# Two chunks' score matmuls on one weight tile in a gated linear attention head, keys packed by GpSimd

## The reference

```
f   = lb + (1 - lb) * sigmoid(fp);  k = 1 - f;  q = silu(q)
per position t, state S (128 x 128):  S = diag(f_t) S + k_t v_t^T;   o_t = q_t S
prompt: S starts at 0, t = 0..511;    samples: S is the carried state, one step each
```

## Time and profile before

| | |
|---|---|
| median of 3 runs | 1100.36 us (1100.23 to 1102.1) |
| profiled execution, span from first to last instruction | 1098.3 us |
| profiled execution, its own time | not shown apart; the median is 2.06 above the span |
| TensorE busy | 1055.9 us, 96% of the span |
| VectorE, ScalarE, GpSimd busy | 573.2, 434.1, 2.9 us |
| mean granted TensorE clock | 0.992 of full |
| moved by DMA | 100.36 MB, 91 GB/s over the span |

### The profile page before, as it was taken

One profiled execution on the slowest core, in us unless ns is written; L12 is line 12 of the kernel. 1 busy time (PEld: TensorE's weight loads), 2 busy tenths in 40 slices (PEclk: granted clock), 3 DMA queues, 4 the chain that ended last, 5 costly groups with the idle time before them and its releaser, 6 DMA issues.

```text
span 1098.3 us, 21670 instructions
## 1 busy us (share of the span) xinstructions
PE 1055.9 (96%) x8542; PEld 1034.8 (94%) x8542; DVE 573.2 (52%) x1028; ACT 434.1 (40%) x588; POOL 2.9 (0%) x9
## 2 busy tenths in 40 slices
PE   4899999999999999999999999699999999999997
PEld 3799999999999899999999999699999999999997
DVE  2666566657656788833333333855554554422223
ACT  5434335433442888822222233652323232322222
POOL 0000000000000000000000000000000000000000
PEclk9999999999999899999999999899999999999999
DMA  5533223222332233232333244033233323233321
GB/s 155 162 90 99 79 76 98 86 76 76 94 108 60 81 93 86 78 95 81 91 95 95 88 130 135 20 97 95 80 92 95 95 82 90 67 92 94 94 76 78
DMA packets 182881, 100.36 MB, mean 91 GB/s; under 512 B 3709, under 2 KB 181378, under 8 KB 182594
## 3 DMA queue, kind: packets, MB, share of 16 engines
q1 hardware_dynamic: 164898, 90.87, 27.8%
q10 hardware_dynamic: 17792, 8.91, 2.7%
q0 software_dynamic: 160, 0.15, 0.0%
HBM read 90.79 MB, written 9.13 MB: 91 GB/s over the span
## 4 chain that ended last, share of the span: by engine, by line
PE 90%; DVE 3%; ACT 2%; issue 1%; SPq 1%; DMA 1%; DVEq 0%; ACTq 0%
PE proj L1223 78%; PE pr L1322 5%; PE pi L1371 1%; DMA raw<-in_w_in 1%; PE pr L1376 1%; PE pi L1353 1%; PE pr L1345 1%; PE pi L1414 1%; PE pr L1414 1%; PE pi L1359 0%; ACT wh L358 0%; SPq L266 0%; DVE tmp L1122 0%; DVE acts L1110 0%; DVE raw L1202 0%
## 5 line engine op out<-in xcount | busy, mean ns | idle before, releaser
L1223 PE MATMUL proj<-acts,wh 128*128 128x260 f32 x4928 | 810.7, 287 | 15.5 <-DVE acts L1110 9.2
L1223 PEld LDWEIGHTS proj<-acts,wh 128*128 128x128 f32 x4928 | 679.9, 190 | 23.7 <-DVE acts L1110 10.8
L1223 PE MATMUL proj<-acts,wl 128*128 128x260 f32 x2464 | 498.5, 284 | 0.0
L1223 PEld LDWEIGHTS proj<-acts,wl 128*128 128x128 f32 x2464 | 381.9, 190 | 0.0
L720 DVE TENSOR_TENSOR wl<-raw,wh 128x1024 fp32r<-128x1024 f32 (+2 forms) x164 | 190.8, 1163 | 278.7 <-ACT wh L358 278.6
L358 ACT ACTIVATE wh<-raw 128x1024 fp32r<-128x1024 f32 (+2 forms) x164 | 165.6, 1010 | 358.9 <-PE proj L1223 350.5
L1322 PE MATMUL pr<-tmp 128*128 128x64 f32 (+1 forms) x512 | 66.4, 272 | 3.2 <-DVE tmp L947 3.2
L1322 PEld LDWEIGHTS pr<-tmp 128*128 128x128 f32 x512 | 62.9, 192 | 4.0 <-DVE tmp L947 3.4
L805 DVE TENSOR_TENSOR tmp<-tmp 128x256 f32<-128x256 f32 x56 | 23.6, 422 | 25.5 <-PE pr L1322 25.4
L676 ACT ACTIVATE acts<-tmp 128x520 f32 (+1 forms) x21 | 13.4, 639 | 42.4 <-DVE tmp L1170 42.4
L673 ACT ACTIVATE tmp<-tmp 128x520 f32<-128x520 f32 x21 | 13.5, 641 | 40.0 <-DVE tmp L1161 40.0
(11 more groups left out here) (239 smaller groups left out, 721.0 us busy)
## 6 DMA issues: line engine op xcount, KB each, us to landing
raw<-in_w_in SPq DMA_DIRECT2D x64, 512.0 KB, 4.0
raw<-in_w_ffn_in SPq DMA_DIRECT2D x44, 512.0 KB, 3.8
raw<-in_w_ffn_out SPq DMA_DIRECT2D x16, 384.0 KB, 3.1
raw<-in_w_ffn_out SPq DMA_DIRECT2D x16, 320.0 KB, 2.9
tmp<-in_state_hgrn ACTq DMA_DIRECT2D x8, 512.0 KB, 4.1
out<-tmp ACTq DMA_DIRECT2D x8, 512.0 KB, 3.2
raw<-in_w_branch_a SPq DMA_DIRECT2D x8, 512.0 KB, 3.6
raw<-in_w_branch_b SPq DMA_DIRECT2D x8, 512.0 KB, 3.5
```

The source lines that it names most:

```text
L1223: o = mm(pp[par][:, hf, 0:TH], w, x[:, hf * TH:(hf + 1) * TH], start=start and n == 0, stop=stop and n == 2)
```

## The change

1. *Scores.* For levels 1 to 7 two chunks share one weight tile. POOL copies, per level, the 256 first-half keys of all chunks into a packed tile `KP` (two tiles of 128 columns: 64 keys of one chunk, 64 of another). The score of a level is then two matmuls of 128 keys by 128 queries instead of four of 128 by 64. `score` also waits for the copy (`k_pack`), and POOL's copy for the key product (`d_k1`), which DVE now does first in a level, ahead of the total and the query product, and on which the next level waits too.
2. *Layout.* So that one access pattern reaches both, the second 256 positions of `QP`, `KS`, `VT`, `FF`, `AT` lie in reverse order; `columns`, `BLOCK` and `back` undo that where order matters. Three evacuations are therefore made in three pieces instead of one (values and forget gate on ACT, queries on DVE). Masks have two variants per level: the loaded table grows from 576 to 1024 columns.
3. *PSUM.* The two halves of a projection result lie next to each other across the bank border, so that `proj` is one run of 520 columns.
4. *Samples.* `STOK` and `VBD` have 128 rows instead of 24; rows 24 to 127 are zeroed once by POOL at the start, and `outer` multiplies over all 128.

The diff, cut to what the text speaks of (matching replacements of `halves(X)` by `X` elsewhere are left out):

```diff
-        def proj(par):
-            return pp[par][:, :, 0:TH]
+        def proj(par, at=0, n=T):
+            return pp[par][:].rearrange("p a n -> p (a n)")[:, 512 - TH + at:512 - TH + at + n]
+        def view(ap, off, *dims):
+            return bass.AP(ap.tensor, ap.offset + off, [list(ap.ap[0])] + [list(d) for d in dims])
+        def back(ap, lo, hi):
+            return view(ap, hi - 1, (-1, hi - lo))
...
-        VBD, STOK = spare[0:NS, 0:NB * P], spare[0:NS, NB * P:(NB + 2) * P]
+        VBD, STOK = spare[:, 0:NB * P], spare[:, NB * P:(NB + 2) * P]
+        KP = extra[:, 0:TC]
...
+        def second_of(ap, b):
+            return view(ap, b, (TC - b, 2), (2 * b, TC // (2 * b)), (1, b))
+        def first_of(ap, b):
+            return view(ap, 0, (TC + b, 2), (2 * b, TC // (2 * b)), (1, b))
+        BLOCK = (0, 1, 3, 2)
+        def columns(ap, c):
+            return ap[:, c * P:(c + 1) * P] if c < 2 else back(ap, BLOCK[c] * P, (BLOCK[c] + 1) * P)
...
         @block.gpsimd
         def _(eng):
+            eng.memset(spare[:, 0:(NB + 2) * P].bitcast(F32), 0.0).then_inc(E("sp_zero"), 1)
+            def pack(h, i):
+                if i == 1:
+                    eng.wait_ge(E("d_f"), h + 1)
+                else:
+                    eng.wait_ge(E("d_k1"), h * 7 + (i - 1))
+                hs = 1 << (i - 1)
+                eng.tensor_copy(KP.rearrange("p (n two b) -> p n two b", two=2, b=hs),
+                   view(KS, 0, (2 * hs, P // hs), (TC + hs, 2), (1, hs))).then_inc(E("k_pack"), 1)
+            for h in range(NH):
+                for i in range(1, 8):
+                    pack(h, i)
...
-                act(halves(VT), proj(0), AF.Copy).then_inc(posted(0), 1)
+                act(VT[:, 0:TC], proj(0, 0, TC), AF.Copy)
+                act(back(VT, TC, TP), proj(0, TC, TC), AF.Copy)
+                act(VT[:, TP:T], proj(0, TP, NB), AF.Copy).then_inc(posted(0), 1)
...
-                act(halves(SIG), proj(0), AF.Sigmoid).then_inc(posted(2), 1)
+                act(SIG[:, 0:TC], proj(0, 0, TC), AF.Sigmoid)
+                act(back(SIG, TC, TP), proj(0, TC, TC), AF.Sigmoid)
+                act(SIG[:, TP:T], proj(0, TP, NB), AF.Sigmoid).then_inc(posted(2), 1)
...
             def level(h, i):
...
-                    tb = tot(b).rearrange("p (n two) -> p n two", two=2)
-                    q2, k1 = cols_of(QP[:, 0:TP], b)[:, :, 1, :], cols_of(KS[:, 0:TP], b)[:, :, 0, :]
+                    n, m = TC // (2 * b), TC // b
+                    tb, t2 = tot(b), tot(b).rearrange("p (n two) -> p n two", two=2)
+                    k1 = first_of(KS, b)
                     if i > 2:
                         ch.wait()
+                        eng.wait_ge(E("d_k1"), h * 7 + i - 2)
                     eng.wait_ge(E("d_L"), h * 8 + i - 1)
                     eng.wait_ge(E("d_take"), h * 8 + i - 1)
-                    ch.link(tt(q2, q2, tb[:, :, 0:1].to_broadcast([P, n, b]), MUL))
-                    ch.link(tt(tot(2 * b), tb[:, :, 0], tb[:, :, 1], MUL))
-                    tt(k1, k1, tb[:, :, 1:2].to_broadcast([P, n, b]), MUL).then_inc(E("d_L"), 1)
+                    tt(k1, k1, view(tb, 1, (m - 1, 2), (2, n), (0, b)), MUL).then_inc(E("d_k1"), 1)
+                    ch.link(tt(tot(2 * b), t2[:, :, 0], t2[:, :, 1], MUL))
+                    tt(second_of(QP, b), second_of(QP, b), view(tb, 0, (m + 1, 2), (2, n), (0, b)), MUL).then_inc(E("d_L"), 1)
                 take(i - 1)
...
-                tt(halves(QP), proj(1), halves(SIG), MUL).then_inc(posted(1), 1)
+                tt(QP[:, 0:TC], proj(1, 0, TC), SIG[:, 0:TC], MUL)
+                tt(back(QP, TC, TP), proj(1, TC, TC), SIG[:, TC:TP], MUL)
+                tt(QP[:, TP:T], proj(1, TP, NB), SIG[:, TP:T], MUL).then_inc(posted(1), 1)
...
             def score(h, i, prev=True):
...
+                    eng.wait_ge(E("k_pack"), h * 7 + i)
                     eng.wait_ge(E("d_L"), h * 8 + i)
...
-                n = P if i == 0 else P // 2
-                for k in range(NCH):
-                    rhs = QP[:, k * P:(k + 1) * P]
-                    if i:
-                        rhs = rhs.rearrange("p (n two b) -> p n two b", two=2, b=1 << (i - 1))[:, :, 1, :]
-                    o = mm(bank[:, k * n:(k + 1) * n], KS[:, k * P:(k + 1) * P], rhs, start=True, stop=True)
+                if i == 0:
+                    for k in range(NCH):
+                        o = mm(bank[:, k * P:(k + 1) * P], KS[:, k * P:(k + 1) * P], QP[:, k * P:(k + 1) * P], start=True, stop=True)
+                else:
+                    hs = 1 << (i - 1)
+                    n = P // (2 * hs)
+                    for k in range(2):
+                        queries = view(QP, k * P + hs, (TC - hs, 2), (2 * hs, n), (1, hs))
+                        o = mm(view(bank, k * P // 2, (P, 2), (1, P // 2)), KP[:, k * P:(k + 1) * P], queries, start=True, stop=True)
                 o.then_inc(E("p_L"), 1)
```

More of the change, by code:

```diff
@@ L424, in hg_steps @@
                     eng.wait_ge(E("d_f"), h)
-                    act(halves(SIG), proj(1), AF.Sigmoid).then_inc(E("a_sg"), 1)
+                    act(SIG, proj(1), AF.Sigmoid).then_inc(E("a_sg"), 1)
                 if not prev:
@@ L440, in hg_steps @@
                     eng.wait_ge(posted(1), 2 * h)
-                act(halves(SIG), proj(1), AF.Sigmoid).then_inc(E("a_sq"), 1)
+                act(SIG, proj(1), AF.Sigmoid).then_inc(E("a_sq"), 1)
                 if prev:
@@ L605, in branch_gate @@
                 eng.wait_ge(posted(1), j * 2 + 2 * G_MIX - 1 + part)
-                act(halves(U(2 * part)), proj(0), AF.Sigmoid).then_inc(posted(0), 1)
+                act(U(2 * part), proj(0), AF.Sigmoid).then_inc(posted(0), 1)
             def mix(j):
@@ L785, in _ @@
             eng.wait_ge(E("m_made"), NLEV)
-            def cols_of(ap, b):
-                return ap.rearrange("p (n two b) -> p n two b", two=2, b=b)
             def level(h, i):
@@ L880, in out_gate @@
                 eng.wait_ge(E("a_sg"), h + 1)
-                tt(halves(SOG), proj(1), halves(SIG), MUL).then_inc(posted(1), 1)
+                tt(SOG, proj(1), SIG, MUL).then_inc(posted(1), 1)
             def lower_bound():
@@ L991, in gelu @@
                 eng.wait_ge(E("d_hl"), n)
-                stt(halves(GG), halves(GSQ), 1.0, proj(1), ADD, MUL).then_inc(posted(1), 1)
+                stt(GG, GSQ, 1.0, proj(1), ADD, MUL).then_inc(posted(1), 1)
             def gated(n):
@@ L1074, in mix @@
                 eng.wait_ge(E("unit_done"), u0 + 2)
-                tt(halves(U(1)), proj(1), halves(U(0)), MUL).then_inc(posted(1), 1)
+                tt(U(1), proj(1), U(0), MUL).then_inc(posted(1), 1)
                 prep(u0 + 3, 3)
@@ L1081, in mix @@
                 eng.wait_ge(E("a_mhi"), j)
-                tt(halves(U(3)), proj(1), halves(U(2)), MUL).then_inc(posted(1), 1)
+                tt(U(3), proj(1), U(2), MUL).then_inc(posted(1), 1)
                 prep(u0 + 5, 1)
@@ L1137, in _ @@
             eng.wait_ge(E("unit_done"), 4 * G_FFI + 2)
[L1138 to L1139 removed]
+            cp(U(0), proj(0)).then_inc(posted(0), 1)
+            cp(U(3), proj(1)).then_inc(posted(1), 1)
             prep(4 * G_FFI + 3, 3)
@@ L1334, in turn_keys @@
             def turn_keys(h):
+                eng.wait_ge(E("d_k1"), h * 7 + 7)
                 eng.wait_ge(E("d_L"), h * 8 + 8)
@@ L1536, in _level_masks @@
         tc = np.arange(P // 2)[None, :]
-        t = tc // hs * 2 * hs + hs + tc % hs
-        m = (s // (2 * hs) == t // (2 * hs)) & (s % (2 * hs) < hs)
-        out.append(m.astype(np.float32))
+        t = tc // hs * 2 * hs + tc % hs
+        same = s // (2 * hs) == t // (2 * hs)
+        out.append((same & (s % (2 * hs) < hs)).astype(np.float32))
+        out.append((same & (s % (2 * hs) >= hs)).astype(np.float32))
     return np.ascontiguousarray(np.concatenate(out, axis=1))
```

63 lines of the change are left out of this document (33 added, 30 removed).

## The result

The changed kernel takes 1094.84 us (median of four runs, 1093.56 to 1095.81) against 1100.3: 5.5 us less, a ratio of 0.9947 with a 95% interval of [0.9932, 0.9963]. The forecast was 1087.3, 13.1 faster. Direction and range held; less than half of the gain came.

The account below looks back on a forecast made before the run. TensorE was taken to bound the eight heads. Scores (-8.0) and outer products (-5.1) took 13.1 us off the span of 1098.3, giving 1085.2; with 2.06 added, the time was 1087.3, range 1081 to 1107.

Parts of the forecast that it names:

- The outer products: Outer products over 128 rows: 0.25 us each for 0.43, pairs behind them back to 1.50; 0.64 a head, 5.1 in all.
- The score itself: Levels 1 to 7: four records for eight, a score costing 0.41 us where it was 0.81.
- wide-score rival: Scores of levels 1 to 7: stepped columns cost double, a score stays at 0.81 us; 1103 in all; chance 0.08.
- Level 4: Behind VectorE's half of the weight split: key product at 8.11, score at 9.36 after score 0, TensorE still for 0.95 us.
- K: Time from the key product's start until TensorE sees packed keys: 1.25 us, bounds 0.96 and 1.51.
- the chain behind a score: Score to next score where TensorE waits: 0.92 us to VectorE's start plus K, 2.17; used for scores 6 and 7.
- The rest of the level hides beside the pack.: In each level, total and query product run beside POOL's pack; queries are ready 0.96 to 1.22 us after the key product's start.
- The start and the hop: VectorE starts 0.92 us after a score, 0.10 of it for the added wait; each hop between engines takes 0.12.
- One sign of failure that was named: The forecast fails if TensorE waits for POOL at each of levels 2 to 7.
- The first rival: At each level the pack can't run beside VectorE and waits for the query product: 1098.6, or 1091 with a 0.40 pack; chance 0.30.
- The long pack: POOL's pack is long: each 0.1 us of K beyond 1.25 costs about 0.4 a head, up to 1109.7; chance 0.17.
- The rest at nothing: Split evacuations, query pieces, larger masks and contiguous PSUM views cost nothing; uncovered, each would cost 0.15 to 0.3 us a head.

Follow-up runs that it names:

- order alone: The kernel before with 128-row outer products and the best kernel's order of VectorE's work, but eight-record scores and no packing: 1095.28 us, ratio 0.9955.
- two-column copy: The changed kernel with each of POOL's packing copies cut to two columns, so the keys aren't packed: 1087.17 us, ratio 0.9876.
- scores alone: The changed kernel with the outer products put back to 24 rows: 1098.88 us, ratio 0.9978 to the kernel before.

## Why the prediction was half right

**What bounds the kernel: right.** Where TensorE's own work was cut and nothing else held it, time went: 0.74 to 0.79 a head with the outer products. Where only feeding it was rearranged, nothing came (order alone).

**The outer products: right, slightly small.** 0.64 a head was forecast and 0.74 came, in the loop. The matmul was priced at 0.25 and took 0.23, the pairs at 1.50 and took 1.44 and 1.45.

**The score itself: right.** From 171.29 to the projection behind it at 171.74 is 0.45 where 0.41 was forecast; the other scores take 0.43 to 0.56. Twice 64 stepped columns cost about what 128 columns in a row do. The wide-score rival falls.

**Level 4: right in what holds it, 0.29 late.** ScalarE's half of the split ends 6.89 after score 0 (6.90 forecast), the key product starts at 8.28 (8.11), and TensorE stands still 0.72 by its matmuls and 0.90 by its weight loads (0.95). Score 4 comes 9.65 after score 0 (9.36): 0.17 of the delay is VectorE's, which is late from level 3 and starts its half of the split later, and 0.12 is a K of 1.37 there.

**The step that failed** is the chain behind a score, 0.92 + K with K = 1.25: a step of 2.17 that turned out to be 2.34, as long as it was before the change. Of the 1.00 that the scores should have gained in a head, 0.14 came in the loop. At level 6 VectorE starts 0.99 after the score, not 0.92; from the key product's start to the pack's it is 0.49, not 0.55; the pack takes 0.62, not 0.58; and TensorE starts 0.24 after it, not 0.12. Two parts of the working were wrong:

- *"The rest of the level hides beside the pack."* Pack and VectorE's products don't run side by side at their own lengths; they take turns. At levels 4 to 7 the pack grows from 0.40 to between 0.61 and 0.67. That the price of 0.58 lies near this is luck: it was the middle between two distant rows, and a pack that runs freely would have made K 1.07 by the same terms. At levels 2 and 3 it is the product that grows, by 0.2, with all of VectorE's queue behind it, so scores 2 and 3 come 0.15 and 0.32 later than forecast.
- *The start and the hop.* The hop of 0.12 was taken from VectorE to ScalarE, and a start of 0.92 was charged 0.10 for one more wait. In the loop they came 0.12 and 0.07 longer, which is more than the 0.17 by which the step was missed; in the last head, with fixed numbers in the waits, they were 0.11 and 0.75, and the same long packs cost TensorE nothing.

Of the 0.88 by which score 7 ends later than forecast, 0.32 are there by score 3, 0.49 come in the steps to scores 5, 6 and 7, and 0.10 in score 7 itself; level 4 gives back 0.03. One sign of failure that was named came in substance: TensorE is late at each of levels 2 to 7, at 2 and 3 for the query product that the pack stretched, from 4 on for the pack.

The first rival, given 0.30, comes nearest, in the version with a pack of 0.40: its K is 1.37, it said 1091, and 1092.4 and 1094.8 came. It has the turn-taking, but it let the pack start when the product ends, while the trace shows it starting beside it and ending 0.26 after it; and its hop is too short for the loop. The Trainium skill (SBUF — State Buffer, "Who interferes with whom") states that a VectorE instruction with two SBUF inputs contends with a GpSimd one that reads SBUF, and that one with at most one SBUF input outside the two-port modes doesn't. The traces agree on the first: 0.62 against 0.40, and a two-column copy held to the product's end. They fit the second: beside the predicated copy, whose data come from PSUM, the pack took 0.40.

**The long pack falls:** no pack took over 0.67. By the figures of the Trainium skill (GPSIMD Engine Reference, sections 3.1 and 7) I had estimated 0.38 to 0.62; 0.40 was measured from runs of 4 elements up and 0.42 with runs of 2, beside the predicated copy, and 0.51 to 0.52 with single elements at level 1.

**The rest at nothing:** no run isolates the split evacuations and the query pieces. In the loop the scores alone gain 0.17 a head, and from score 0 to the end of score 7 it is 0.14, so nothing large hides there.

## What to carry to other kernels

When an engine's step gets shorter, price the path that feeds it as a chain, hops included; here it was already as long as the old step, and in the loop the shortening paid only once the pack was out of that chain. Take the price of a wait from rows of the same loop: 0.37 of this chain was gone in the one head whose waits had fixed numbers. For the same reason, look at a mean over heads head by head: over half of the scores' gain came from the last. Work moved to an idle GpSimd isn't free of VectorE: where both read SBUF, add their times, or have GpSimd do it a level ahead, or let the producer write the final layout. A part that looks like a by-product can carry the gain, so time the parts apart, and on a measure that leaves out what varies between executions.

## What was not expected of the hardware

**The clock after the passage.** In the passage to the second branch TensorE waits 1.62 us, and runs the next stretch at a granted clock of 0.50, the lower of its two levels (1.2 GHz). Windows of 4 us (length, busy time of PE, PEld, DVE, ACT, POOL, then the granted clock, the DMA share and GB/s), the first of them 4 us after the last head's first outer product, of the changed kernel in its two executions:

```profile
345.96:349.96 4.00, 2.79 (x16) 2.79 (x16) 1.76 (x6) 0.00 (x0) 0.00 (x0) 0.73 0.45 131
349.96:353.96 4.00, 4.00 (x16) 3.48 (x16) 0.69 (x1) 2.58 (x4) 0.00 (x0) 0.50 0.46 147
353.96:357.96 4.00, 4.00 (x30) 3.48 (x30) 0.96 (x3) 2.77 (x4) 0.00 (x0) 0.92 0.00 0
```

```profile
345.32:349.32 4.00, 2.79 (x24) 2.79 (x25) 1.76 (x6) 0.67 (x2) 0.00 (x0) 0.99 0.45 131
349.32:353.32 4.00, 4.00 (x17) 2.97 (x17) 0.69 (x1) 2.73 (x4) 0.00 (x0) 0.58 0.49 147
353.32:357.32 4.00, 4.00 (x34) 3.96 (x33) 2.00 (x4) 3.05 (x6) 0.00 (x0) 1.00 0.00 0
```

After the same wait the clock falls earlier in the first and stays low longer; the same 16 matmuls take 3.03 and 1.95 us. From the last head's first outer product to the second group of gate matmuls in the second branch it is 25.4 to 25.6 us in seven of the profiled executions and 23.7 to 23.9 in the other seven, among them one of each for the changed kernel. So 1.6 us of a comparison of two profiles can be the moment at which the clock falls, and none of the change. What picks the one or the other is open.

**A 24-row matmul costs more than a 128-row one** of the same columns: 0.43 against 0.23, and 0.2 more in the pair behind it. The weight loads show where: behind the 24-row matmul's start (159.11) the next weight load starts after 0.42, behind the 128-row one's (157.89) after 0.08.
